# Token-major gate and output projections in the first block's mixers, with the merged result turned on TensorE

## The chip, the cores and the metric

One core of one Trainium2 chip. The metric is the device time of one execution in microseconds, as the median of a few runs. The kernel before was run three times: 1937.15 to 1938.6 us, median 1938.12 us.

## The reference

A model of 256 tokens and width 1024: two layers of a first block, then two of a second one. The change is in the mixer of the first block, so only that part is given:

```
h = rmsnorm(x, mix_norm_pre[l])
z = h @ w_in[l]
aq, ak, av, mq, mk, mv, mo, mi, mf, gl = jnp.split(z, SPLIT_IDX, axis=-1)
ya = diff_attention(aq, ak, av, lam, lam_init, attn_norm_w[l])
...
ym = (jax.nn.sigmoid(mo) * rmsnorm(hm, mlstm_norm_w[l]).reshape(b_, s_, M_V))
g_a, g_m = jnp.split(jax.nn.sigmoid(gl + gate_b[l]), 2, axis=-1)
merged = g_a * (ya @ w_proj_a[l]) + g_m * (ym @ w_proj_m[l])
x = x + rmsnorm(merged @ w_out[l], mix_norm_post[l])
```

`gl` is 256 x 2048, `ya`, `ym` and `merged` are 256 x 1024, and `hm` is the output of a chunkwise mLSTM with 8 heads of 128 values each.

## The kernel before

Every weight matrix is streamed through the core once, in 623 units of 128 x 1024 values (512 KB). SyncE loads a unit into a ring of four (`w_raw`). ScalarE rounds it into `w_hi` (line 572) and VectorE takes the rest, `w_raw` minus `w_hi`, into `w_lo` (line 1094); both rings hold six units. A matrix product is then three passes on TensorE: high part by high part, high by low and low by high. ScalarE splits unit u once unit u-6 is used up (`unit_done`), so the two splitting engines run up to five units ahead of TensorE.

There are two ways to use a unit.

- Feature-major (`product`, lines 1854 to 1856, called by `model_unit`): a 128 x 128 tile of the weights is loaded into the array and 256 tokens stream past. A unit is 24 matmuls of 256 columns, and its result, 128 features x 256 tokens, is finished in one unit, in a third of the way round three PSUM banks (`out_bank`).
- Token-major (`tokens`, lines 1860 to 1862, called by `chunk`): a 128 x 128 tile of the activations (128 tokens, 128 of the inner dimension) is loaded and 512 columns of weights stream past. A unit is 12 matmuls of 512 columns, and four units make a chunk: 512 features for the two halves of the tokens, in two banks (`tok_bank`).

A mixer is 88 units, numbered here 0 to 87 from its start, as the variable `i` of the loops in the code: values of the attention (0 to 7, token-major), queries, keys and convolution inputs (8 to 31, feature-major), output gate and values of the mLSTM (32 to 47, token-major), `gl` (48 to 63), `ya @ w_proj_a` (64 to 71) and `ym @ w_proj_m` (72 to 79), all 32 of them feature-major, and `merged @ w_out` (80 to 87, with `merged` as the array's side). In the listing these starts are `U_MO` 32, `U_GL` 48, `U_PA` 64, `U_PM` 72 and `U_OUT` 80.

Each engine has a program of its own, and its order is that of the `for i in range(U_QK, U_OUT)` loop in that engine's block. In its step i, TensorE first does the small work that is due (scores of mLSTM head (i-48)/2 on even i, values on odd i, the transposes of `ym_turn`), then unit i. ScalarE and VectorE split unit i+5 in their step i and do the small work that belongs to i. All waits are semaphores: an engine that waits holds up everything behind it in its own program.

The mLSTM heads run in three groups, 0 to 2, 3 to 5 and 6 and 7. For a group ScalarE copies the numerators out of PSUM (`take_num`, line 754) and squares them, VectorE computes denominators and variances (`mlstm_stats`), ScalarE the reciprocal root (`mlstm_rstd`), and VectorE scales the heads into `ym_tok` (`mlstm_out`, line 1394). There is one copy of `num`, so `take_num` of a group waits for the `ym_ready` of all heads before it. Then TensorE turns the heads two by two into bank 3 (`ym_turn`, line 2153), and ScalarE and VectorE split them out of it (`ym_round`, line 772; `ym_rest`, line 1404). `ym_turn(p)` waits until the pair before has left the bank (`ym_split`).

The gates are scaled by the row norm out of PSUM (line 1474), put through the sigmoid with a bias for each partition (line 836), multiplied with the projections (line 1412), added (1416) and split (843, 1418).

Of the kernel before, what the change touches and what calls it, by code (L numbers as in the profile page):

```python
# [5 lines left out]
F32 = mybir.dt.float32  # L6
# [37 lines left out]
for _name, _n in (("attn_norm", 1), ("one_minus_lam_init", 1), ("lam_init", 1),  # L44
                  ("mlstm_norm", HEADS), ("conv_w", 32), ("conv_b", 8), ("gate_b", 16), ("lam", 4),
                  ("igate_b", 1), ("fgate_b", 1), ("w_gates", KT * 64)):
    C1[_name] = _at
    _at += _n
# [10 lines left out]
NPAR = max(N1, N2)  # L59

# [13 lines left out]
NC = _at  # L74


def build(nc, x, consts, gains, params, w_up1, w_down1, w_mix1, w_mix2, w_up2, w_down2, out):
    with ExitStack() as ctx:
# [73 lines left out]
        gl, _ = sb("gates_merge", [P, 16, T])  # L152
# [191 lines left out]
        gl_scaled = sem("gl_scaled")  # L344
# [46 lines left out]
        proj_done = sem("proj_done")  # L391
# [57 lines left out]
        def conv_at(l):  # L449
# [4 lines left out]
        TOK_FIRST = (0, 4, U_MO, U_MO + 4, U_MV, U_MV + 4)  # L454
        tok_bank = ((bank[0], bank[1]), (side[0], side[1]), (bank[2], bank[0]), (bank[1], bank[2]),
                    (bank[0], bank[1]), (bank[2], bank[0]))
        GROUPS = ((0, 3), (3, 6), (6, 8))
        YA_TURN = (25, 27, 35, 37)
        YM_TURN = (57, 63, 65, 68)
# [86 lines left out]
        def _(act):  # L546
# [119 lines left out]
            def mixer(l):  # L666
# [3 lines left out]
                def store(c, dst):  # L670
                    for t in range(QT):
                        if t == 0:
                            act.wait_ge(chunk_out, l * 6 + c + 1)
# [100 lines left out]

                for j in range(8):
                    hi_next()
# [7 lines left out]
                for i in range(U_QK, U_OUT):  # L784
# [48 lines left out]
                    if 65 <= i < 69:  # L833
                        for m in range(4 * (i - 65), 4 * (i - 64)):
                            act.wait_ge(gl_scaled, l * 16 + m + 1)
                            nc.scalar.activation(gl[:, m], gl[:, m], ACT.Sigmoid,
                                                 bias=p1("gate_b", m)).then_inc(gl_sig, 1)
                    if i == 70:
                        exp_set()
                    if i >= U_PM:  # L840
                        m = i - U_PM
                        act.wait_ge(proj_done, l * 24 + 8 + 2 * (m + 1))
                        nc.scalar.activation(h_hi[:, m], gl[:, m], ACT.Copy).then_inc(mix_hi, 1)
                for i in range(U_OUT, U_MIX - 2):
                    hi_next()
                post_norm(n, u0 + U_MIX - 1, n + 1)
# [91 lines left out]
            def mixer2(l):  # L938
# [52 lines left out]
                def take_gelu(t):  # L991
                    if t == 0:
                        act.wait_ge(chunk_out, DEPTH * 6 + l * 2 + 1)
# [4 lines left out]
                def take_values(t):  # L998
                    if t == 0:
                        act.wait_ge(chunk_out, DEPTH * 6 + l * 2 + 2)  # L1000
# [51 lines left out]
            for l in range(DEPTH):  # L1052
                ffn(l, 0)

                act.wait_ge(par_in, l * 16 + 16)
                mixer(l)
                ffn(l, 1)
            for l in range(DEPTH):
                nc.scalar.preload_act_table_set("gelu_and_others")

                act.wait_ge(par_in, l * 16 + 16 * (DEPTH + 1))
# [7 lines left out]
        def _(dve):  # L1069
# [134 lines left out]
            def mixer(l):  # L1204
# [179 lines left out]
                def mlstm_out(g):  # L1384
# [7 lines left out]
                    for h in range(a, z):  # L1392
                        for t in range(QT):
                            r = nc.vector.scalar_tensor_tensor(
                                out=ym_tok[:, t, h * P:(h + 1) * P], in0=num[:, t, h - a, 0:P],
                                scalar=m_rs[:, t, h - a:h - a + 1], in1=mo_tok[:, t, h * P:(h + 1) * P],
                                op0=ALU.mult, op1=ALU.mult)
                        r.then_inc(ym_ready, 1)
# [9 lines left out]
                def proj(i):  # L1408
                    m = i - U_PA
                    dve.wait_ge(gl_sig, l * 16 + m + 1)  # L1410
                    dve.wait_ge(unit_done, u0 + i + 1)
                    nc.vector.tensor_tensor(gl[:, m], gl[:, m], out_bank(i), ALU.mult).then_inc(proj_done, 1)
                    if i >= U_PM:
                        m = i - U_PM
                        dve.wait_ge(proj_done, l * 24 + 8 + 2 * m + 1)
# [1348 lines left out]
```

## Time and profile before

| | before |
|---|---|
| median of 3 runs | 1938.12 us (1937.15 to 1938.6) |
| time of the profiled execution | 1937.21 us |
| its span | 1935.0 us |
| busy TensorE matmul, weight load, VectorE, ScalarE | 99%, 86%, 67%, 58% |
| units 48 to 79, first mixer | 356.95 to 465.77 us, 108.82 us |
| the same, second mixer | 1025.25 to 1134.0 us |
| granted TensorE clock, mean | 0.999 |

The span is what the profiler saw of the one execution, 2.2 us less than its time. All positions below are microseconds from the start of the span. 

The durations of matmul records overlap, since matmuls are pipelined. What a matmul costs is read from the distance between starts, not from its duration.

### The profile page before, as it was taken

Reading aid. Unit: us, or ns where it says so; the run is one execution under the profiler, and the core shown is the slowest. Engines: PE = TensorE matmul, PEld = TensorE weight load, DVE = VectorE, ACT = ScalarE, POOL = GpSimd, SP = SyncE. Lnnn points to the kernel's source line nnn. Section 1 sums busy time; section 2 is a strip of 40 time slices with the busy share of each in tenths; the row PEclk is TensorE's granted clock in tenths of the full one; section 3 lists DMA queues with packets and bytes.
Section 4 is the critical chain, followed back from the end, with each engine's and each line's share of the span. In section 5 each row is a group of like instructions: output and inputs, shape, how many; then the busy total and the mean of one; then the engine's idle time right before and its main releaser. Section 6 shows DMA issues by size and latency. Waiting matters only on the chain.

```text
span 1935.0 us, 28373 instructions
## 1 busy us (share of the span) xinstructions
PE 1922.7 (99%) x10936; PEld 1660.8 (86%) x10936; DVE 1303.2 (67%) x2243; ACT 1123.9 (58%) x1798; POOL 6.5 (0%) x18
## 2 busy tenths in 40 slices
PE   9999999999999999999999999999999999999998
PEld 7888899999888888888989998888988888988887
DVE  5555887566755575558865666555858888858886
ACT  6444766564644564456774655445747666647665
POOL 0000000000000000000000000000000000000000
PEclk9999999999999999999999999999999999999999
DMA  8655445546566555655455446664536555536553
GB/s 285 192 186 185 163 137 169 163 132 198 192 190 189 174 185 185 187 161 174 142 166 163 153 162 218 187 190 153 171 113 187 183 187 179 172 111 188 183 187 97
DMA packets 93684, 335.74 MB, mean 174 GB/s; under 512 B 10224, under 2 KB 12528, under 8 KB 93552
## 3 DMA queue, kind: packets, MB, share of 16 engines
q1 hardware_dynamic: 92688, 329.49, 54.1%
q0 software_dynamic: 720, 4.37, 0.6%
q8 instruction: 87, 1.43, 0.3%
q14 instruction: 45, 0.37, 0.1%
q10 hardware_dynamic: 144, 0.09, 0.0%
HBM read 332.86 MB, written 1.05 MB: 173 GB/s over the span
## 4 chain that ended last, share of the span: by engine, by line
PE 94%; DVE 5%; ACT 1%; issue 0%; DMA 0%; SPq 0%; DVEq 0%; ACTq 0%
PE stream L1860 10%; PE stream L1862 10%; PE stream L1861 10%; PE acc L1860 9%; PE acc L1862 9%; PE acc L1861 9%; PE stream L1854 7%; PE stream L2344 7%; PE stream L1855 7%; PE stream L1856 7%; PE stream L2345 3%; PE stream L1956 1%; DVE w_lo L1094 1%; PE acc L2270 1%; PE acc L2067 1%; DVE conv_tiles L1559 1%
## 5 line engine op out<-in xcount | busy, mean ns | idle before, releaser
L1094 DVE TENSOR_TENSOR w_lo<-w_raw,w_hi 128x1024 fp32r<-128x1024 f32 x623 | 757.9, 1223 | 363.6 <-ACT w_hi L572 362.1
L572 ACT ACTIVATE w_hi<-w_raw 128x1024 fp32r<-128x1024 f32 x623 | 653.4, 1054 | 372.5 <-PE stream L1862 206.8
L1860 PE MATMUL stream<-w_hi,h_both 128*128 128x512 f32 x896 | 354.0, 395 | 0.0
L1862 PE MATMUL stream<-w_lo,h_both 128*128 128x512 f32 x896 | 349.1, 390 | 0.0
L1861 PE MATMUL stream<-w_hi,h_both 128*128 128x512 f32 x896 | 348.9, 389 | 0.0
L1854 PE MATMUL stream<-h_both,w_hi 128*128 128x256 f32 x800 | 234.4, 293 | 0.0
L1856 PE MATMUL stream<-h_both,w_lo 128*128 128x256 f32 x800 | 226.0, 283 | 0.0
L1855 PE MATMUL stream<-h_both,w_hi 128*128 128x256 f32 x800 | 226.0, 283 | 0.0
L2344 PE MATMUL stream<-h_both,w_hi 128*128 128x512 f32 x608 | 217.4, 400 | 0.0
L1860 PE MATMUL acc<-w_hi,act_hi 128*128 128x512 f32 x528 | 211.2, 400 | 1.6 <-DVE conv_sums L1551 1.3
L1862 PE MATMUL acc<-w_lo,act_hi 128*128 128x512 f32 x528 | 206.3, 391 | 0.0
L1861 PE MATMUL acc<-w_hi,act_lo 128*128 128x512 f32 x528 | 206.0, 390 | 0.0
L1860 PEld LDWEIGHTS stream<-w_hi,h_both 128*128 128x128 f32 x896 | 168.3, 188 | 35.8 <-DVE w_lo L1094 1.0
L1862 PEld LDWEIGHTS stream<-w_lo,h_both 128*128 128x128 f32 x896 | 168.2, 188 | 35.6
L1861 PEld LDWEIGHTS stream<-w_hi,h_both 128*128 128x128 f32 x896 | 168.4, 188 | 33.1
L2345 PE MATMUL stream<-h_both,w_lo 128*128 128x256 f32 x608 | 170.7, 281 | 0.0
L1854 PEld LDWEIGHTS stream<-h_both,w_hi 128*128 128x128 f32 x800 | 152.8, 191 | 4.0 <-issue 0.8
L1855 PEld LDWEIGHTS stream<-h_both,w_hi 128*128 128x128 f32 x800 | 153.0, 191 | 0.1
L1856 PEld LDWEIGHTS stream<-h_both,w_lo 128*128 128x128 f32 x800 | 152.8, 191 | 0.0
L2344 PEld LDWEIGHTS stream<-h_both,w_hi 128*128 128x128 f32 x608 | 114.2, 188 | 26.9
L1860 PEld LDWEIGHTS acc<-w_hi,act_hi 128*128 128x128 f32 x528 | 99.2, 188 | 23.9 <-issue 2.6
L1862 PEld LDWEIGHTS acc<-w_lo,act_hi 128*128 128x128 f32 x528 | 99.1, 188 | 21.8
(336 smaller groups left out, 2614.7 us busy)
## 6 DMA issues: line engine op xcount, KB each, us to landing
w_raw<-in_w_up SPq DMA_DIRECT2D x264, 512.0 KB, 3.5
w_raw<-in_w_mix SPq DMA_DIRECT2D x228, 512.0 KB, 3.5
w_raw<-in_w_down SPq DMA_DIRECT2D x132, 512.0 KB, 3.5
params<-in_params POOLq DMA_DIRECT2D x4, 859.5 KB, 6.4
x_residual<-in_x SPq DMA_DIRECT2D x4, 256.0 KB, 5.6
out_x<-x_residual SPq DMA_DIRECT2D x4, 256.0 KB, 2.5
constants<-in_consts POOLq DMA_DIRECT2D x1, 832.0 KB, 7.2
constants<-in_consts SPq DMA_DIRECT2D x1, 192.0 KB, 8.0
```

Of the source, the lines that this page charges most:

```text
L572: nc.scalar.activation(w_hi[:, u % RING], w_raw[:, u % RAW], ACT.Copy).then_inc(hi_ready, 1)
L1094: nc.vector.tensor_tensor(w_lo[:, u % RING], w_raw[:, u % RAW], w_hi[:, u % RING].bitcast(F32), ALU.subtract).then_inc(split_done, 1)
L1559: r = nc.vector.scalar_tensor_tensor(out=cbuf[:, s, back:], in0=conv_src(i, side_i)[:, 0:T - back], scalar=p2("conv_w", ((2 - back) * 2 + ...
L1854: nc.tensor.matmul(dst, w_hi[:, s, w], hi, start=first, stop=False)
L1855: nc.tensor.matmul(dst, w_hi[:, s, w], lo, start=False, stop=False)
L1856: return nc.tensor.matmul(dst, w_lo[:, s, w], hi, start=False, stop=last)
L1860: nc.tensor.matmul(dst, hi, w_hi[:, s, w], start=first, stop=False)
L1861: nc.tensor.matmul(dst, lo, w_hi[:, s, w], start=False, stop=False)
L1862: return nc.tensor.matmul(dst, hi, w_lo[:, s, w], start=False, stop=last)
L1956: r = nc.tensor.transpose(dst, cbuf[:, 2 * (c % 2) + t, half(i)], ident)
L2344: nc.tensor.matmul(dst, w_hi[:, u % RING, w], h_both[:, k], start=(k == 0), stop=False)
L2345: r = nc.tensor.matmul(dst[:, 0:T], w_lo[:, u % RING, w], h_hi[:, k], start=False, stop=(k == KT - 1))
```

## The change

The 16 units of `gl`, the 8 of `w_proj_a` and the 8 of `w_proj_m` are packed as `wide` units on the host and used token-major: eight more chunks (6 to 13) of four units. `out_bank` is no more used for them, and chunk c takes the next two of banks 0 to 2. The results lie token-major in `gl`, so:

- VectorE takes each chunk in two pieces of 128 x 512, with a bias that now varies along the row (`gl_take`), which is loaded as 2 x 1024 values for each partition: half of it into `params`, half over constants that only the second block uses, which are loaded later. The first piece is taken when the first token half of the chunk is done (`chunk_out`, half way through the chunk's last unit), before VectorE's split in that step; the second one after it, with a wait for the unit's end.
- The sigmoid is four instructions of 128 x 1024 in steps 65, 67, 70 and 73, where there were 16 of 128 x 256 in steps 65 to 68.
- `merged` is token-major and `w_out` needs its transpose: eight 128 x 128 transposes ahead of unit 78 and eight ahead of unit 82 (`merged_turn`), each eight split by two ScalarE and two VectorE instructions.
- `mlstm_out` is called by head, in steps 55, 57, 61, 63 and 65, where it was called by group in 55, 61 and 65. The first two `ym_turn` move from 57 and 63 to 60 and 64, the third from 65 to 66.

```diff
-        YM_TURN = (57, 63, 65, 68)
+        HEADS_OUT = {55: (0,), 57: (1, 2), 61: (3, 4), 63: (5,), 65: (6, 7)}
+        SIGMOID_AT = (65, 67, 70, 73)
+        YM_TURN = (60, 64, 66, 68)
+        MERGE_TURN = (78, 82)
...
+                def gl_take(c, t):
...
+                    if t == 0:
+                        dve.wait_ge(chunk_out, l * TOK_CHUNKS + c + 1)
+                    else:
+                        dve.wait_ge(unit_done, u0 + TOK_FIRST[c] + 4)
+                    nc.vector.scalar_tensor_tensor(out=gl[:, t, cols_c], in0=tok_bank[c][t][:],
+                                                   scalar=rs_all[:, T + t:T + t + 1], in1=b, op0=ALU.mult,
+                                                   op1=ALU.add).then_inc(gl_taken, 1)
...
+                    taking = i >= U_GL and i % 4 == 3
+                    if taking:
+                        chunk_take(GL_CHUNK + (i - U_GL) // 4, 0)
                     lo_next()
+                    if taking:
+                        chunk_take(GL_CHUNK + (i - U_GL) // 4, 1)
...
-                        if i == U_GL + 3 + 2 * (z - 1):
-                            mlstm_out(g)
+                    if i in HEADS_OUT:
+                        for h in HEADS_OUT[i]:
+                            mlstm_out(h)
...
+                def merged_turn(a):
+                    for t in range(QT):
+                        pe.wait_ge(merged_in, l * 4 + 2 * a + t + 1)
...
+                        for j in range(4):
+                            r = nc.tensor.transpose(bank[3 - t][:, blk(j)],
+                                                    gl[:, t, (4 * a + j) * P:(4 * a + j + 1) * P], ident)
+                        r.then_inc(merged_turned, 1)
...
-                    if i < U_PA:
-                        model_unit(out_bank(i), u, h_hi, h_lo)
...
+                    model_unit(out_bank(i), u, h_hi, h_lo)
```

Three places show how the engines' programs change. The first is VectorE's program in steps 62 to 65 of the first mixer; before:

```order
L1358 SCALAR_TENSOR_TENSOR mlstm_p<-acc,decay 128x384 [waits num_ready,mlstm_qk,mw_ready]
L1474 TENSOR_TENSOR gates_merge<-stream,mix_rstd 128x256 [waits unit_done]
L1094 TENSOR_TENSOR w_lo<-w_raw,w_hi 128x1024 [waits hi_ready]
L1404 SCALAR_TENSOR_TENSOR ym_lo<-stream,params,ym_hi 128x256 [waits ym_hi_done] x2
L1474 TENSOR_TENSOR gates_merge<-stream,mix_rstd 128x256 [waits unit_done]
L1094 TENSOR_TENSOR w_lo<-w_raw,w_hi 128x1024 [waits hi_ready]
L1367 SCALAR_TENSOR_TENSOR mlstm_den<-mlstm_num 128x2x2 [waits num_taken]
L1371 TENSOR_TENSOR mlstm_den<-mlstm_den,e_cols 128x2x2 [waits dve_step]
L1374 RECIPROCAL mlstm_rec<-mlstm_den 128x2x2 [waits m_stat]
L1376 TENSOR_REDUCE mlstm_var<-mlstm_num_squares 128x2x2 [waits num_squared]
```

and the same place of the changed kernel, where `L1113` is the split, `L1442` the taking of a chunk's piece and `L1419` a head's scaling:

```order
L1377 SCALAR_TENSOR_TENSOR mlstm_p<-acc,decay 128x384 [waits num_ready,mlstm_qk,mw_ready]
L1442 SCALAR_TENSOR_TENSOR gates_merge<-stream,mix_rstd,constants 128x512 [waits chunk_out]
L1113 TENSOR_TENSOR w_lo<-w_raw,w_hi 128x1024 [waits hi_ready]
L1442 SCALAR_TENSOR_TENSOR gates_merge<-stream,mix_rstd,constants 128x512 [waits unit_done]
L1419 SCALAR_TENSOR_TENSOR ym_tok<-mlstm_num,mlstm_rs,out_gate_tok 128x128 x2
L1113 TENSOR_TENSOR w_lo<-w_raw,w_hi 128x1024 [waits hi_ready]
L1386 SCALAR_TENSOR_TENSOR mlstm_den<-mlstm_num 128x2x2 [waits num_taken]
L1390 TENSOR_TENSOR mlstm_den<-mlstm_den,e_cols 128x2x2 [waits dve_step]
L1393 RECIPROCAL mlstm_rec<-mlstm_den 128x2x2 [waits m_stat]
L1395 TENSOR_REDUCE mlstm_var<-mlstm_num_squares 128x2x2 [waits num_squared]
L1397 TENSOR_TENSOR mlstm_var<-mlstm_var,mlstm_rec 128x2x2 [waits m_stat]
L1400 TENSOR_TENSOR mlstm_var<-mlstm_var,mlstm_rec 128x2x2 [waits m_stat]
```

Head 5 is now scaled in step 63, behind both pieces of chunk 9, and the pair of `ym_lo` splits has moved from step 63 to behind the statistics of step 64 (its row follows the last one shown). The second place is ScalarE's program in steps 63 to 65; before:

```order
L754 ACTIVATE mlstm_num<-acc 128x260 [waits ym_ready,num_ready]
L754 ACTIVATE mlstm_num<-acc 128x260
L757 ACTIVATE mlstm_num_squares<-mlstm_num 128x2x256 [waits num_taken]
L772 ACTIVATE ym_hi<-stream,params 128x256 [waits ym_turned]
L772 ACTIVATE ym_hi<-stream,params 128x256
L572 ACTIVATE w_hi<-w_raw 128x1024 [waits unit_done,raw_full3]
L763 ACTIVATE mlstm_rs<-mlstm_var,eps_72 128x2x2 [waits m_stat]
L766 ACTIVATE mlstm_rs<-mlstm_rs 128x2x2 [waits act_step]
```

and after the change, where `L766` is the copy of the numerators, `L584` the split, `L775` and `L778` the reciprocal root and `L784` the rounding of a turned head:

```order
L766 ACTIVATE mlstm_num<-acc 128x260 [waits ym_ready,num_ready]
L766 ACTIVATE mlstm_num<-acc 128x260
L769 ACTIVATE mlstm_num_squares<-mlstm_num 128x2x256 [waits num_taken]
L584 ACTIVATE w_hi<-w_raw 128x1024 [waits unit_done,raw_full3]
L775 ACTIVATE mlstm_rs<-mlstm_var,eps_72 128x2x2 [waits m_stat]
L778 ACTIVATE mlstm_rs<-mlstm_rs 128x2x2 [waits act_step]
L784 ACTIVATE ym_hi<-stream,params 128x256 [waits ym_turned]
L784 ACTIVATE ym_hi<-stream,params 128x256
```

The rounding of heads 2 and 3 stood ahead of the wait for the variances and now stands behind it. The third place is TensorE's program at the start of unit 78 of the changed kernel, where nothing stood between units 77 and 78 before:

```order
L1924 MATMUL stream<-w_lo,ym_hi 128x512
L2242 MATMUL stream<-constants,gates_merge 128x128 [waits ym_split,merged_in]
L2242 MATMUL stream<-constants,gates_merge 128x128 x3
L2242 MATMUL stream<-constants,gates_merge 128x128 [waits merged_in]
L2242 MATMUL stream<-constants,gates_merge 128x128 x3
L1922 MATMUL stream<-w_hi,ym_hi 128x512 [waits split_done]
```

Eight transposes were put in, in two waits of four.

## Rows read from the trace of the kernel before

**Rows 1.** Page, part 1: busy time and share of the span by engine.

```profile
PE 1922.7 (99%) x10936; PEld 1660.8 (86%) x10936; DVE 1303.2 (67%) x2243; ACT 1123.9 (58%) x1798; POOL 6.5 (0%) x18
```

**Rows 2.** Page, part 4: the chain that ended last, by engine.

```profile
PE 94%; DVE 5%; ACT 1%; issue 0%; DMA 0%; SPq 0%; DVEq 0%; ACTq 0%
```

**Rows 3.** Windows: units 48 to 79, 40 to 46 (token-major), 69 to 76 (feature-major).

```profile
356.95:465.77 108.82, 108.82 (x889) 105.81 (x888) 69.20 (x126) 57.71 (x95) 0.00 (x0) 1.00 0.50 149
335.20:354.24 19.04, 19.04 (x86) 15.77 (x85) 8.49 (x7) 13.51 (x14) 0.00 (x0) 1.00 0.66 202
434.10:457.14 23.04, 23.04 (x195) 23.04 (x194) 16.34 (x25) 11.82 (x18) 0.00 (x0) 1.00 0.67 199
```

**Rows 4.** Timeline of TensorE: where steps 62 to 66 start.

```profile
410.77 0.34 PE L2116 MATMUL acc<-neg_keys_rounded,ident_rounded 128*128 128x384 f32 x1
...
414.86 0.38 PE L2139 MATMUL acc<-mlstm_v_tok,mlstm_p 128*128 128x130 f32 x2
...
421.73 0.60 PE L2153 MATMUL stream<-constants,ym_tok 128*128 128x128 f32 x4
...
425.03 0.28 PE L1854 MATMUL stream<-ya_hi,w_hi 128*128 128x256 f32 x1
```

**Rows 5.** Timeline of TensorE: 12 token-major matmuls with four, and with eight, transposes.

```profile
320.66 0.60 PE L2102 MATMUL stream<-constants,o_normed 128*128 128x128 f32 x4
...
323.84 0.39 PE L1860 MATMUL stream<-w_hi,h_both 128*128 128x512 f32 x1
...
485.52 0.39 PE L1860 MATMUL acc<-w_hi,h_both 128*128 128x512 f32 x1
...
489.15 0.39 PE L1860 MATMUL acc<-w_hi,h_both 128*128 128x512 f32 x1
```

**Rows 6.** Lines: VectorE's split, a 128x512 piece from PSUM, a head's scaling, mLSTM weights.

```profile
L1094 DVE TENSOR_TENSOR w_lo<-w_raw,w_hi 128x1024 fp32r<-128x1024 f32 x623 | 757.9, 1223 | 363.6 <-ACT w_hi L572 362.1
...
L1336 DVE SCALAR_TENSOR_TENSOR ya_lo<-stream,attn_norm_scaled,ya_hi 128x512 fp32r<-128x512 f32 x8 | 6.0, 748 | 7.8 <-ACT ya_hi L730 7.8
...
L1394 DVE SCALAR_TENSOR_TENSOR ym_tok<-mlstm_num,mlstm_rs,out_gate_tok 128x128 f32<-128x128 f32 x32 | 8.9, 346 | 0.2
...
L1358 DVE SCALAR_TENSOR_TENSOR mlstm_p<-acc,decay 128x384 f32<-128x384 f32 x16 | 8.8, 551 | 0.0
```

**Rows 7.** Timeline of ScalarE, steps 63 to 65.

```profile
416.08 0.65 ACT L754 ACTIVATE mlstm_num<-acc 128x260 f32<-128x260 f32 x2
...
417.30 0.82 ACT L772 ACTIVATE ym_hi<-stream,params 128x256 fp32r<-128x256 f32 x2
...
422.92 0.30 ACT L763 ACTIVATE mlstm_rs<-mlstm_var,eps 128x4 f32<-128x4 f32 x1 [2.76 <-DVE mlstm_var L1381]
...
423.36 1.04 ACT L572 ACTIVATE w_hi<-w_raw 128x1024 fp32r<-128x1024 f32 x1
424.31 0.82 ACT L772 ACTIVATE ym_hi<-stream,params 128x256 fp32r<-128x256 f32 x2
425.14 1.28 ACT L836 ACT_TABLE_LOAD   x1
```

**Rows 8.** Timeline of VectorE, steps 62 to 64.

```profile
415.06 0.42 DVE L1474 TENSOR_TENSOR gates_merge<-stream,mix_rstd 128x256 f32<-128x256 f32 x1 [0.64 <-PE stream L1856]
...
418.16 0.88 DVE L1404 SCALAR_TENSOR_TENSOR ym_lo<-stream,params,ym_hi 128x256 fp32r<-128x256 f32 x2 [0.72 <-ACT ym_hi L772]
...
420.20 1.23 DVE L1094 TENSOR_TENSOR w_lo<-w_raw,w_hi 128x1024 fp32r<-128x1024 f32 x1 [0.73 <-ACT w_hi L572]
421.34 0.16 DVE L1367 SCALAR_TENSOR_TENSOR mlstm_den<-mlstm_num 128x4 f32<-128x4 f32 x1
```

**Rows 9.** The span's end: TensorE's last transposes, then windows with the granted clock.

```profile
1929.36 1.23 PE L2265 MATMUL stream<-constants,y_tok 128*128 128x128 f32 x8 [2.79 <-ACT y_tok L864]
...
1929.50:1930.00 0.50, 0.50 (x6) 0.50 (x6) 0.00 (x0) 0.00 (x0) 0.00 (x0) 1.00 0.00 0
1930.00:1930.50 0.50, 0.50 (x5) 0.21 (x2) 0.00 (x0) 0.45 (x2) 0.00 (x0) 0.68 0.00 0
```

In the window rows the columns are: stretch, its length, busy time (and instructions) of TensorE, its weight load, VectorE, ScalarE and GpSimd, granted clock of TensorE, busy share of the DMA engines, GB/s. In the rows of lines: busy us in total, mean ns of one, idle time before them.

More of the change, by code:

```diff
@@ L773, in ym_round, with merged_round @@
                                              scale=p1("mlstm_norm", 2 * p + j)).then_inc(ym_hi_done, 1)
+                def merged_round(a):
+                    for t in range(QT):
+                        act.wait_ge(merged_turned, l * 4 + 2 * a + t + 1)
+                        nc.scalar.activation(h_hi[:, 4 * a:4 * a + 4, half(t)],
+                                             bank[3 - t][:].rearrange("p (k q) -> p k q", k=4),
+                                             ACT.Copy).then_inc(mix_hi, 1)
                 for j in range(8):
@@ L832, in mixer @@
                         ym_round(YM_TURN.index(i))
[L833 to L838, printed above, removed]
+                    if i in SIGMOID_AT:
+                        c = SIGMOID_AT.index(i)
+                        act.wait_ge(gl_taken, l * 16 + 2 * (c + 1))
+                        x = gl[:, :, 512 * c:512 * (c + 1)]
+                        nc.scalar.activation(x, x, ACT.Sigmoid).then_inc(gl_sig, 1)
+                    if i == SIGMOID_AT[-1] + 1:
                         exp_set()
[L840 to L843, printed above, removed]
+                    if i in MERGE_TURN:
+                        merged_round(MERGE_TURN.index(i))
                 for i in range(U_OUT, U_MIX - 2):
                     hi_next()
+                    if i in MERGE_TURN:
+                        merged_round(MERGE_TURN.index(i))
                 post_norm(n, u0 + U_MIX - 1, n + 1)
@@ L1391, in mlstm_out @@
                         dve.wait_ge(mo_ready, l + 1)
[L1392 to L1398, printed above, removed]
+                def mlstm_out(h):
+                    for g, (a, z) in enumerate(GROUPS):
+                        if h == a:
+                            mlstm_scales(g)
+                        if a <= h < z:
+                            at = h - a
+                    for t in range(QT):
+                        r = nc.vector.scalar_tensor_tensor(
+                            out=ym_tok[:, t, h * P:(h + 1) * P], in0=num[:, t, at, 0:P],
+                            scalar=m_rs[:, t, at:at + 1], in1=mo_tok[:, t, h * P:(h + 1) * P],
+                            op0=ALU.mult, op1=ALU.mult)
+                    r.then_inc(ym_ready, 1)
                 def ym_rest(p):
@@ new lines, in chunk_take, with merged_rest @@
+                def chunk_take(c, t):
+                    if c < PA_CHUNK:
+                        gl_take(c, t)
+                    else:
+                        proj_take(c, t)
+                def merged_rest(a):
+                    for t in range(QT):
+                        dve.wait_ge(mix_hi, l * 4 + 2 * a + t + 1)
+                        nc.vector.tensor_tensor(h_lo[:, 4 * a:4 * a + 4, half(t)],
+                                                bank[3 - t][:].rearrange("p (k q) -> p k q", k=4),
+                                                h_hi[:, 4 * a:4 * a + 4, half(t)].bitcast(F32),
@@ L2653, in mix1 @@
     heads = np.stack([tiles(a) for a in (q, k)], axis=1).reshape(2 * HEADS, P, D)
[L2654 to L2655 removed]
+    return np.concatenate([wide(va), heads, tiles(mqk)]
+                          + [wide(a) for a in (mo, mv, gl[:, 0:D], gl[:, D:], v["w_proj_a"][l], v["w_proj_m"][l])]
                           + [v["w_out"][l].reshape(KT, P, D)])
```

142 lines of the change are left out of this document (82 added, 60 removed).

## The prediction

> **What bounds the kernel now.** I read the page first: TensorE is busy 99% of the span, VectorE 67%, ScalarE 58% [rows 1], and the chain that ended last runs on TensorE for 94% [rows 2]. Then the windows of the changed place: in units 48 to 79 TensorE is busy for all of the 108.82 us at a granted clock of 1.00, VectorE for 69.2 and ScalarE for 57.7 of them, the DMA engines half the time [rows 3]. So TensorE never waits there, and the time moves in two ways only: by what TensorE is given to do, and by a wait that comes anew. VectorE and ScalarE have room, and work taken from them is worth nothing in itself. It is their order that counts.
>
> **Less matmul time.** A unit has 6144 columns in either form. Eight feature-major units took 23.04 us, 2.88 each; seven token-major ones took 19.04 us, 2.72 each [rows 3]. Per matmul that is 23.04 / 192 = 0.120 us for 256 columns and 19.04 / 84 = 0.227 us for 512: each costs some 13 ns more than its columns at 2.4 GHz, and a token-major unit has 12 fewer of them. 32 units in each of two mixers save 64 x 0.16 = 10.2 us.
>
> One rule speaks against this saving. The Trainium skill ("TensorE: Matmul & The Clock Gate", section "Wait — 56ns, not 53.3ns?") gives a warm matmul its columns over 2.4 GHz plus about 2.5 ns. By it the units would take 24 x 109.2 and 12 x 215.8 ns, 0.03 us apart, and the 64 would save 1.9 us in place of 10.2. The rows of this kernel decide, since both forms run here with the same operand types [rows 3].
>
> **New transposes.** The 16 transposes of a mixer come in two batches of eight. Twelve token-major matmuls with eight transposes among them took 489.15 - 485.52 = 3.63 us [rows 5], 0.91 more than 2.72. Four batches: +3.6 us. They turn another tile but are the same fp32 128 x 128 operation. By twice the cost of four transposes, below, a batch would be 0.84 to 0.92, so the bounds are 3.4 and 3.7.
>
> **Small work among larger matmuls.** Four transposes ahead of a unit cost 425.03 - 421.73 - 2.88 = 0.42 us in feature-major surroundings [rows 4] and 323.84 - 320.66 - 2.72 = 0.46 in token-major ones [rows 5]. 0.03 to 0.04 more at each of 20 places (eight scores, eight values, four head turns) in two mixers is +1.4; two fewer changes of form give some back. I take +1.0 (0 to 1.6).
>
> **What lies beside.** VectorE's two pieces of a chunk (748 ns each for such a shape [rows 6]) replace four of about 420 ns, four sigmoids replace 16, and the split of `merged` shrinks from eight instructions to four on either engine. None was waited for [rows 3], so all this is nothing. The added bias loads are 1 MB beside 336 MB, on GpSimd's queue, with a whole FFN to arrive in. The banks: a chunk's first piece is taken at the half of its last unit and its bank is needed 2.7 us later, and the split of turned results at unit 78 has until unit 80; both have more than a microsecond left.
>
> **The wait that comes anew.** In step 63 the changed order makes a ring. ScalarE's copy of the third group's numerators waits for head 5, and VectorE scales head 5 only after both pieces of chunk 9; and `ym_turn(2)` ahead of unit 66 waits for the split of heads 2 and 3, which now stands behind the third group's statistics on VectorE and behind its reciprocal root on ScalarE. Before, head 5 was ready in step 61 and the split of step 63 stood ahead of the statistics. The clock of the chain starts at 0 when the second half of unit 63 starts:
> - the signal reaches VectorE 0.20 later (415.06 after 414.86) [rows 4, 8]; first piece of chunk 9, 0.67 to the next start (748 ns long [rows 6], less the 0.08 by which the split's 1.23 exceeds the 1.14 to the next start [rows 8]); split of unit 68, 1.14; second piece, 0.67; head 5 in two instructions of 0.35 [rows 6], the first again 0.08 less: at 3.30 head 5 is ready
> - ScalarE starts 0.04 later; numerators and squares, 1.22 to the next start (416.08 to 417.30 [rows 7]); split of unit 69, 1.04 [rows 7]: 5.60
> - VectorE's half of unit 69 starts 0.04 later, 1.14; statistics up to ScalarE's root 1.58 (421.34 to 422.92 [rows 7, 8]): 8.36
> - root, 0.44 to the next start; rounding of two heads 0.82 [rows 7]; 0.04, and the rest of them 0.88 [rows 8]: 10.54.
>
> TensorE meanwhile needs 1.36 for the rest of unit 63, 0.46 for `ym_turn(1)` [rows 5] and 2 x 2.72: it stands before `ym_turn(2)` at 7.26. With 0.1 for the signal the wait is 10.64 - 7.26 = 3.4 us. It could be 2.6, if pieces and hand-overs run faster, or 4.2. Before, nothing of this was near: heads 0 to 5 were scaled in good time, and the wait for the variances (2.76 us on ScalarE [rows 7]) stood behind the rounding. Both mixers: +6.8 us (5.2 to 8.4). It does not spread: five units are split ahead of TensorE, and `ym_turn(3)` comes at 10.64 + 0.46 + 2 x 2.72 = 16.5. ScalarE is free at 8.36 + 0.44 + 0.82 = 9.6, and up to there it and VectorE need a split (1.04), a table load (1.28), a sigmoid of a split's size (1.04), a split (1.04), a rounding (0.82) and a rest (0.92) [rows 7, 8]: 15.8, 0.7 early.
>
> Another place is close. Head 4's weights must be ready for unit 57. From the half of unit 55 VectorE has 0.20, a piece 0.67, a split 1.14, a piece 0.67, head 0 with its small product 0.73, a split 1.14 and the weights 0.55 [rows 6, 8]: 5.1. TensorE has 1.36, and a scores step of 414.86 - 410.77 = 4.09 [rows 4] less 0.16: 5.3. I count no wait, with 0.3 in each mixer as the upper bound.
>
> **Sum.** -10.2 + 3.6 + 1.0 + 6.8 = +1.2 us on the profiled execution: a span of 1936.2 and a time of 1938.4. That execution's 1937.21 is 0.9 below the median of the runs, so the median goes from 1938.12 to 1939.3. The lower bounds together give 1936.5, the upper ones (3.7, 1.6, 8.4 and 0.6 for unit 57) 1942.2.
>
> **The rivals.**
> - *No wait.* The chain above is cut somewhere (ScalarE does not come to depend on head 5, say) and TensorE never stands at unit 66. Then -5.6: 1932.5. For it: TensorE did not wait at any place of these units before. Against: the chain is 3.3 us too long, all of its lengths but the pieces of chunk 9 come from this same stretch, and no step of it can be passed by an engine that keeps its order. To get below 1934.2 the wait must shrink under 0.9 us. Chance 0.10.
> - *The clock falls, slower.* At the span's end the last dense matmul ended about 1926.56, TensorE stood for 2.79 us, and eight transposes ran from 1929.36; the granted clock was 1.00 up to 1930.0 and 0.68 on average in the half microsecond after, so it went from 2.4 to 1.2 GHz about 3.6 us after the dense work ended [rows 9]. A wait of 3.4 us followed by four transposes is close to that. No row shows how long the lower clock would stay under dense work; as an estimate, if as long as it took to fall, half of 3.6 us is lost each time. One fall of the two: 1941.1; both: 1942.9, which is slower. It decides once TensorE is without dense matmuls for about as long as there, so from a wait of some 3.2 us with the four transposes behind it. Chance that it makes the kernel slower by more than 0.2%: 0.15; that one fall leaves it within: 0.25. The Trainium skill (same page, section "Why this matters for your kernels") advises against idle gaps between bursts of matmuls, since the clock goes back to its lower level; the end of this trace agrees.
> - *Columns alone count.* If a matmul's time were its columns, both forms of a unit would take 6144 / 2.4 GHz = 2.56 us, the change would save nothing on them, and the 3.6 + 1.0 + 6.8 would be left: 1949.5, slower. Against it stand the 2.88 and 2.72 us [rows 3]. Chance 0.01. The Trainium skill's rule above comes near to it, with 1947.6.
> - *More waits.* Unit 57 and `ym_turn(3)` both wait after all: 0.3 to 1 us each in each mixer, 1940 to 1943. Chance 0.06.
>
> **How the numbers follow.** A measurement of this kernel tells changes of over 0.2% (3.9 us) from none: faster is below 1934.2, slower above 1942.0. My forecast, with the wait at unit 66 and the clock kept or lost once at most, has 0.68. Faster: 0.10 of no wait and 0.01 of a short one, 0.11. Slower: 0.15 clock, 0.01 rule, 0.03 of more waits, 0.19. Same: 0.70. The range reaches down to the lower bounds of the terms, less the 1 us by which executions of one kernel differ, 1935.5, leaving out no wait (0.10), and up to both falls of the clock, 1943.3, leaving out under 0.05.
>
> **What would show it.** In the changed profile: token-major units of 2.72 us all through steps 48 to 79; two groups of eight transposes for each mixer costing 0.9; a wait of TensorE of about 3.4 us ahead of unit 66 in both mixers, ended by VectorE's rest of the turned heads, and ScalarE's copy of numerators waiting on VectorE's scaling of head 5; units 48 to 79 in about 108.82 - 5.1 + 0.9 + 0.5 + 3.4 = 108.5 us (the second batch of transposes is behind them). A granted clock under 1.00 there would be the second rival. The prediction is wrong if TensorE stands anywhere else for more than half a microsecond, or nowhere.

## The result and the profile after

The changed kernel takes 1943.53 us (median of 9 runs, 1941.71 to 1945.73), the kernel before beside it 1937.38 (9 runs, 1937.06 to 1938.6). The ratio is 1.003, with a 95% interval of 1.0022 to 1.0039: slower by 0.3%, past the 0.2% that the prediction took as the least that can be told. The difference is +6.2 us, where +1.2 was forecast. The time is 0.2 us above the upper end of the predicted range (1943.3), which the interval of the ratio takes in. The profiled execution took 1944.23, its span is 1942.4 (1935.0 before).

The page of the changed kernel, part 1, then part 4 by engine, beside [rows 1, 2]:

```profile
PE 1923.0 (99%) x10200; PEld 1627.1 (84%) x10200; DVE 1297.1 (67%) x2195; ACT 1119.5 (58%) x1766; POOL 8.1 (0%) x21
...
PE 91%; DVE 6%; ACT 1%; issue 1%; DMA 0%; DVEq 0%; ACTq 0%
```

736 matmuls fewer, and yet TensorE is busy for as long as before (1922.7). By the prediction's own terms for its work (-10.2, +3.6, +1.0) it would be busy for 5.6 us less, so this is the first hint at a slower clock. The waits of TensorE over the whole span (engine, tile and line waited for; us in total, times, longest):

```profile
PE stream L2220 <- DVE ym_lo L1429: 6.5, 2, 3.2
PE stream L2334 <- ACT y_tok L883: 3.3, 4, 2.8
PE stream L2622 <- DVE ln_half L1840: 1.5, 1, 1.5
PE acc L1922 <- DVE conv_sums L1610: 1.3, 2, 0.7
PE acc L2511 <- DVE qk L1732: 1.0, 2, 0.7
```

The first row is new, one wait in each mixer, at `ym_turn(2)` ahead of unit 66. The last one was a single wait of 0.12 us before. The others stood in the kernel before with the same sizes. Windows of the changed kernel: units 48 to 79 of the first and of the second mixer (columns as in [rows 3]), where it was 108.82 us in both [rows 3]:

```profile
357.38:467.94 110.56, 107.32 (x513) 87.18 (x512) 66.44 (x104) 55.68 (x80) 0.00 (x0) 0.98 0.48 153
1028.22:1139.89 111.67, 108.43 (x513) 88.16 (x512) 66.45 (x104) 55.68 (x80) 0.00 (x0) 0.97 0.47 152
```

Less work (TensorE was busy for all 108.82), and the granted clock is under 1.00. Where it is lost, the shorter windows show, behind the wait in the first mixer and then in the second, where the first row ends within the wait and the next one lies wholly in it:

```profile
423.00:426.60 3.60, 0.36 (x4) 0.30 (x4) 2.13 (x7) 2.54 (x6) 0.00 (x0) 1.00 0.45 146
426.60:428.00 1.40, 1.40 (x8) 1.18 (x7) 1.36 (x4) 1.39 (x2) 0.00 (x0) 0.75 0.00 0
428.00:430.00 2.00, 2.00 (x6) 1.56 (x5) 1.16 (x4) 2.00 (x4) 0.00 (x0) 0.50 0.67 225
430.00:432.00 2.00, 2.00 (x8) 1.58 (x8) 1.57 (x3) 0.87 (x2) 0.00 (x0) 0.82 0.25 66
...
1093.00:1096.20 3.20, 0.92 (x5) 0.42 (x3) 1.73 (x8) 1.33 (x5) 0.00 (x0) 1.00 0.51 161
1096.20:1096.80 0.60, 0.00 (x0) 0.00 (x0) 0.60 (x2) 0.60 (x1) 0.00 (x0) 0.60 0.04 14
...
1101.00:1103.00 2.00, 2.00 (x6) 1.58 (x5) 1.41 (x3) 0.09 (x1) 0.00 (x0) 0.50 0.27 55
1103.00:1105.00 2.00, 2.00 (x10) 1.59 (x10) 0.20 (x1) 1.58 (x2) 0.00 (x0) 0.96 0.58 229
```

0.50 is 1.2 GHz. In the first mixer the clock fell about 1 us after the work had begun again (426.33) and was low for 3.4 us; in the second it fell 0.84 us before TensorE could go on (1097.16), and was low for 6.8 us:

```profile
427.31:430.72 3.41, 3.41 (x10) 2.64 (x9) 2.54 (x8) 2.94 (x5) 0.00 (x0) 0.50 0.45 154
1096.32:1103.15 6.83, 5.99 (x16) 4.88 (x17) 5.14 (x11) 4.74 (x6) 0.00 (x0) 0.50 0.31 92
```

The timeline of TensorE shows what that does to a matmul of 512 columns: 0.43 from start to start where it is 0.23 at 2.4 GHz.

```profile
422.70 0.39 PE L1924 MATMUL stream<-w_lo,ya_hi 128*128 128x512 f32 x1
426.33 0.63 PE L2220 MATMUL stream<-constants,ym_tok 128*128 128x128 f32 x4 [3.24 <-DVE ym_lo L1429]
426.71 0.48 PE L1922 MATMUL stream<-w_hi,ya_hi 128*128 128x512 f32 x1
...
428.91 0.63 PE L1922 MATMUL stream<-w_hi,ya_hi 128*128 128x512 f32 x1
429.33 0.63 PE L1923 MATMUL stream<-w_hi,ya_lo 128*128 128x512 f32 x1
...
431.14 0.39 PE L1922 MATMUL stream<-w_hi,ya_hi 128*128 128x512 f32 x1
431.37 0.39 PE L1923 MATMUL stream<-w_hi,ya_lo 128*128 128x512 f32 x1
```

The wait itself is the ring that the prediction followed. Its links, from the chain of the changed kernel that ended last (start, us, what):

```profile
415.81 0.75 DVE gates_merge L1442
416.56 1.13 DVE w_lo L1113
417.69 0.66 DVE gates_merge L1442
418.35 0.53 DVE ym_tok L1419 x2
...
418.93 0.04 issue
418.97 0.68 ACT mlstm_num L766 x2
...
420.21 1.05 ACT w_hi L584
421.26 0.02 issue
421.29 1.22 DVE w_lo L1113
...
423.81 0.17 DVE mlstm_var L1400
424.01 0.31 ACT mlstm_rs L775
...
424.81 0.47 ACT ym_hi L784
425.28 0.03 issue
425.31 0.89 DVE ym_lo L1429 x2
```

The second half of unit 63 began at 415.61, so the last row ends some 10.6 after it (predicted 10.54), and the matmul ahead of the wait would have handed over at 422.70 + 0.23 = 422.93, 3.40 before the transposes start (predicted 3.4). ScalarE's copy of the numerators (`L766`) waited 4.09 us for head 5, as foretold.

### The profile page after: what moved, and what is told of

Same layout as the page of the kernel before. It is cut to its first block, busy times and chain, and to the rows that moved or that the text cites. A ratio compares the mean times of both kernels' runs of the same rounds, so it can differ in the third digit from the quotient of the medians.

```text
span 1942.4 us, 26766 instructions
## 1 busy us (share of the span) xinstructions
PE 1923.0 (99%) x10200; PEld 1627.1 (84%) x10200; DVE 1297.1 (67%) x2195; ACT 1119.5 (58%) x1766; POOL 8.1 (0%) x21
## 4 chain that ended last, share of the span: by engine, by line
PE 91%; DVE 6%; ACT 1%; issue 1%; DMA 0%; DVEq 0%; ACTq 0%
PE stream L1922 13%; PE stream L1924 12%; PE stream L1923 12%; PE acc L1922 9%; PE acc L1924 9%; PE acc L1923 9%; PE stream L2413 7%; PE stream L2414 3%; PE stream L1916 3%; PE stream L1917 3%; PE stream L1918 3%; DVE w_lo L1113 2%; PE stream L2018 1%; PE acc L2339 1%; PE acc L2134 1%; DVE conv_tiles L1618 1%
## 5 line engine op out<-in xcount | busy, mean ns | idle before, releaser
L1113 DVE TENSOR_TENSOR w_lo<-w_raw,w_hi 128x1024 fp32r<-128x1024 f32 x623 | 758.8, 1222 | 380.0 <-ACT w_hi L584 378.2
L584 ACT ACTIVATE w_hi<-w_raw 128x1024 fp32r<-128x1024 f32 x623 | 654.5, 1055 | 412.5 <-PE stream L1924 292.3
L1922 PE MATMUL stream<-w_hi,h_both 128*128 128x512 f32 x1024 | 407.1, 398 | 0.0
L1924 PE MATMUL stream<-w_lo,h_both 128*128 128x512 f32 x1024 | 399.4, 390 | 0.0
L1923 PE MATMUL stream<-w_hi,h_both 128*128 128x512 f32 x1024 | 398.7, 389 | 0.0
L1922 PEld LDWEIGHTS stream<-w_hi,h_both 128*128 128x128 f32 x1024 | 192.4, 188 | 41.3 <-DVE w_lo L1113 0.9
L1924 PEld LDWEIGHTS stream<-w_lo,h_both 128*128 128x128 f32 x1024 | 192.2, 188 | 41.1
L1923 PEld LDWEIGHTS stream<-w_hi,h_both 128*128 128x128 f32 x1024 | 192.5, 188 | 37.3
L2414 PE MATMUL stream<-h_both,w_lo 128*128 128x256 f32 x608 | 170.7, 281 | 0.0
L1916 PE MATMUL stream<-h_both,w_hi 128*128 128x256 f32 x544 | 159.1, 292 | 0.0
L1917 PE MATMUL stream<-h_both,w_hi 128*128 128x256 f32 x544 | 153.7, 283 | 0.0
L1918 PE MATMUL stream<-h_both,w_lo 128*128 128x256 f32 x544 | 153.7, 283 | 0.0
L2413 PEld LDWEIGHTS stream<-h_both,w_hi 128*128 128x128 f32 x608 | 114.2, 188 | 26.9
L2414 PEld LDWEIGHTS stream<-h_both,w_lo 128*128 128x128 f32 x608 | 114.9, 189 | 0.8
L1923 PEld LDWEIGHTS acc<-w_hi,act_lo 128*128 128x128 f32 x528 | 99.4, 188 | 17.8
L1916 PEld LDWEIGHTS stream<-h_both,w_hi 128*128 128x128 f32 x544 | 104.0, 191 | 2.0 <-issue 0.8
```

Source lines behind the costliest of these rows:

```text
L584: nc.scalar.activation(w_hi[:, u % RING], w_raw[:, u % RAW], ACT.Copy).then_inc(hi_ready, 1)
L1113: nc.vector.tensor_tensor(w_lo[:, u % RING], w_raw[:, u % RAW], w_hi[:, u % RING].bitcast(F32), ALU.subtract).then_inc(split_done, 1)
L1916: nc.tensor.matmul(dst, w_hi[:, s, w], hi, start=first, stop=False)
L1917: nc.tensor.matmul(dst, w_hi[:, s, w], lo, start=False, stop=False)
L1918: return nc.tensor.matmul(dst, w_lo[:, s, w], hi, start=False, stop=last)
L1922: nc.tensor.matmul(dst, hi, w_hi[:, s, w], start=first, stop=False)
```

## The experiments

The theory: the changed kernel is 6 us slower because of the ring through head 5, which takes 3.4 us of TensorE in each mixer, and because each such stand also costs the clock; without it the change would gain. The rivals: the order is innocent and the chunks' pieces, the forms or the transposes cost more than reckoned; or the clock falls for another reason than the stand. Each kernel was timed beside the kernel before on its chip (medians there 1937.56 to 1937.66). What tells most is one number from the traces, the length of units 48 to 79:

```
                       first   second mixer   TensorE's stands there (first / second)
before                108.82   108.82         none
after                 110.56   111.67         3.24 / 3.24
k1_head5              105.99   106.06         0.31 / 0.30
k2_turn63             110.48   111.54         3.24 / 3.23
k3_fill               108.88   108.94         1.43 / 1.43  (behind 8 filling matmuls)
k4_order_only         110.38   110.38         0.67 + 0.58, both
k5_both               105.88   105.88         0.27 / 0.27
k6_fill3              108.93   110.55         2.57 / 2.57  (behind 3 filling matmuls)
k8_turn_twice         106.78   106.81         0.25 / 0.24
k9_form_proj          107.91   107.88         none
k10_form_all          109.65   109.65         none
```

**k1_head5.** One head out earlier cuts the ring at its first link.

```diff
-        HEADS_OUT = {55: (0,), 57: (1, 2), 61: (3, 4), 63: (5,), 65: (6, 7)}
+        HEADS_OUT = {55: (0,), 57: (1, 2), 61: (3, 4, 5), 65: (6, 7)}
```

> The changed kernel with head 5 scaled in step 61 (with heads 3 and 4) and not in step 63. Nothing else. Theory (the ring of step 63 and the clock that falls behind it cost the time): ScalarE's copy of the last group's numerators no longer waits for VectorE, the chain to the rest of heads 2 and 3 ends 7.6 us after the half of unit 63 where it ended at 10.6, TensorE waits 0.3 to 0.5 us ahead of unit 66 in place of 3.4, and the granted clock is 1.00 all through both mixers. Time 1933.5 to 1935.5 us. Rival (the time is lost elsewhere, in the token-major form or its transposes, and the wait is only where it shows): the gain is at most the 6 us of the waits, 1938 us or more. Rival (the clock falls for another reason than the wait): the clock stays below 1.00 after unit 66 and the time is about 1938.

Measured: 1933.93 us (1932.51 to 1934.4), ratio 0.998 (0.9971 to 0.999). The wait ahead of unit 66 is 0.31 and the clock 1.00 in both stretches:

```profile
357.68:463.67 105.99, 105.68 (x514) 85.97 (x513) 66.24 (x104) 55.54 (x80) 0.00 (x0) 1.00 0.48 159
1023.98:1130.04 106.06, 105.76 (x514) 85.96 (x512) 66.27 (x104) 55.54 (x80) 0.00 (x0) 1.00 0.48 159
```

So one entry of a table is worth 9.6 us against the changed kernel, 4.6 and 5.6 in the two stretches. The waits grew shorter by 2.9 each. The rest, 1.6 and 2.7, is the clock's: it was below 1.00 in both stretches of the changed kernel and is 1.00 here.

**k2_turn63.** The second turn one step earlier, head 5 left where the change put it.

```diff
-        YM_TURN = (60, 64, 66, 68)
+        YM_TURN = (60, 63, 66, 68)
```

> The changed kernel with the turn of heads 2 and 3 ahead of unit 63 and not of unit 64, so that their split stands ahead of the last group's statistics, as before the change; head 5 stays in step 63. Theory of the ring: no wait ahead of unit 66. But ScalarE stays late by its wait for head 5, and the next pair (rounded after unit 71's split and a sigmoid) is out of the bank 15.7 us after the half of unit 63, where TensorE comes to the turn of heads 6 and 7 at 13.2: the wait moves to unit 68 and is about 2.6 us, in both mixers. Without a fall of the clock 1939 us, with one or two 1941 to 1943. Rival (only the order of the split matters, not head 5): no wait at all, 1933 to 1934 us.

Measured: 1942.78 us (1941.23 to 1944.91), ratio 1.0028 (1.0016 to 1.004). The third turn is in time now, and the fourth waits instead, two units later and just as long:

```profile
432.75 0.41 PE L2220 MATMUL stream<-constants,ym_tok 128*128 128x128 f32 x2 [3.24 <-DVE ym_lo L1429]
```

I had expected 2.6. The stand was moved, not shortened: the cause is the late head, not the turn behind which it shows. The clock fell again in both mixers (stretches 110.48 and 111.54).

**k3_fill and k6_fill3.** Eight matmuls of 512 columns (three in k6_fill3) into a bank that is free at that time stand ahead of `ym_turn(2)`. They shorten TensorE's idle time and leave the ring alone.

```diff
+                        if i == 66:
+                            for _ in range(8):
+                                nc.tensor.matmul(side[0][:, 0:512], ya_hi[:, 0, 0:P],
+                                                 ya_hi[:, 0:2].rearrange("p k t -> p (k t)"), start=True, stop=True)
```

> The changed kernel with eight more matmuls of 512 columns (some 1.8 us, into a free bank, their result is overwritten) ahead of the turn before unit 66, inside the wait. The wait's end does not move, only TensorE's idle time falls from 3.2 to about 1.4 us. Theory (the clock is lost through the idle time, and costs what the time lies above 1940): the granted clock is 1.00 through units 48 to 79 in both mixers, the wait still ends at the same place, and the time falls by 3 to 5 us, to 1939 to 1941 us. Rival (the lower clock is not due to the idle time, or costs nothing): the time stays at 1943 us, or rises.

> The changed kernel with three filling matmuls ahead of the turn before unit 66 in place of eight, so that TensorE idles about 2.6 us in each mixer (3.2 without filling, 1.4 with eight). It asks where between 1.4 and 3.2 us the clock begins to fall. Theory (a fall needs about the 3.6 us without dense matmuls of the trace's end): no fall in most executions, 1939.5 to 1940.5 us. Rival (the fall starts soon after 1.4 us of idle time): the clock is below 1.00 in one of the mixers at least, and the time is 1941 us or more.

Measured: 1939.7 us (1938.82 to 1940.22) with eight, ratio 1.0011 (1.0001 to 1.002); 1941.15 (1939.14 to 1942.32) with three, ratio 1.0016 (1.0006 to 1.0025). With eight TensorE idles for 1.43 us, the transposes start as long after the ring began as in the changed kernel, and the clock stays at 1.00 in both stretches:

```profile
357.06:465.94 108.88, 107.45 (x521) 87.56 (x520) 66.27 (x104) 55.54 (x80) 0.00 (x0) 1.00 0.48 156
1026.35:1135.29 108.94, 107.51 (x522) 87.55 (x520) 66.26 (x104) 55.55 (x80) 0.00 (x0) 1.00 0.48 155
```

That is 3.8 us back for work that has no use. The slowest of its ten executions (1940.22) is still faster than the fastest of the changed kernel's nine (1941.71), so probably none of those nine kept the clock in both mixers, though only one of them has a profile. With three TensorE idles for 2.57, and the one profiled execution has both answers, the clock kept in the first mixer and lost in the second (stretches 108.93 and 110.55):

```profile
428.00:431.00 3.00, 3.00 (x15) 2.48 (x14) 2.15 (x5) 3.00 (x5) 0.00 (x0) 1.00 0.53 175
...
1097.00:1099.00 2.00, 2.00 (x6) 1.54 (x5) 1.16 (x5) 2.00 (x3) 0.00 (x0) 0.50 0.59 137
1099.00:1101.00 2.00, 2.00 (x7) 1.59 (x7) 1.85 (x3) 0.87 (x3) 0.00 (x0) 0.67 0.31 125
```

I had expected no fall in most executions and 1939.5 to 1940.5 us; the rival, a fall in one mixer at least and 1941 or more, came true. The spread of its runs (1939.14 to 1942.32) would fit a kernel that loses the clock sometimes. The clock's share is shown by the changed kernel and k3_fill side by side: same order, same ring, the wait ended by the same instruction at the same place, and only the idle time differs.

**k4_order_only.** The kernel before, feature-major as it was, with the new steps for heads and turns alone.

```diff
-        YM_TURN = (57, 63, 65, 68)
+        YM_TURN = (60, 64, 66, 68)
+        HEADS_OUT = {55: (0,), 57: (1, 2), 61: (3, 4), 63: (5,), 65: (6, 7)}
...
-                        if i == U_GL + 3 + 2 * (z - 1):
-                            mlstm_out(g)
+                    if i in HEADS_OUT:
+                        for h in HEADS_OUT[i]:
+                            mlstm_out(h)
```

> The kernel before, feature-major, with the new order of the mLSTM outputs alone: heads scaled in steps 55, 57, 61, 63 and 65, turns ahead of units 60, 64, 66 and 68. Theory (the ring comes from this order, not from the token-major form): by the same steps, with the short evictions of this form, the rest of heads 2 and 3 ends 8.4 us after unit 63 where TensorE stands at 6.2: a wait of about 2.3 us ahead of unit 66 in both mixers, 1942 to 1943 us, the clock at 1.00. Rival (the ring needs the chunk's two pieces on VectorE): no wait, 1938 us.

Measured: 1940.83 us (1940.33 to 1941.35), ratio 1.0016 (1.0007 to 1.0025). Two waits in each mixer, ahead of units 66 and 68, of 0.67 and 0.58 us where I had put 2.3. VectorE's timeline shows why:

```profile
416.27 1.22 DVE L1095 TENSOR_TENSOR w_lo<-w_raw,w_hi 128x1024 fp32r<-128x1024 f32 x1 [0.73 <-ACT w_hi L573]
417.42 0.61 DVE L1401 SCALAR_TENSOR_TENSOR ym_tok<-mlstm_num,mlstm_rs,out_gate_tok 128x128 f32<-128x128 f32 x2
418.66 0.42 DVE L1482 TENSOR_TENSOR gates_merge<-stream,mix_rstd 128x256 f32<-128x256 f32 x1 [0.63 <-PE stream L1864]
```

Here head 5 (`L1401`) stands ahead of the piece that waits for unit 63 (`L1482`), in the changed kernel behind two such pieces and the wait for the unit's end. So the order alone makes a ring of a microsecond; with the pieces of the chunk ahead of the head it makes 3.4. Neither part has it by itself.

**k5_both.** Both moves, head 5 in step 61 and the second turn in step 63.

> The changed kernel with both moves: head 5 scaled in step 61, and the turn of heads 2 and 3 ahead of unit 63. Theory: the rest of heads 2 and 3 is out of the bank 3.5 us after the half of unit 63 and of heads 4 and 5 12.8 us after it, where TensorE comes to its turns at 7.3 and 13.2: no wait ahead of unit 66 or 68, the clock at 1.00, and the time is that with head 5 alone moved (1933.9) less its two waits of 0.45: about 1933 us, 0.2 to 0.3% below the kernel before. Rival (the saving of the token-major form is smaller than 10 us and what was gained came from elsewhere): 1936 us or more.

Measured: 1933.94 us (1932.99 to 1934.74), ratio 0.998 (0.9972 to 0.9989). I had expected no wait and about 1933 us. There is one of 0.27 ahead of unit 68, and the kernel is no better than k1_head5. It is the base of the four kernels that follow.

**k7_bias_late.** Changed kernels reach step 48 of the first mixer 0.1 to 1.0 us later than before. Is that the added bias load at the start? Its second half waits for unit 24 here.

```diff
                     if k == 0:
+                        pool.wait_ge(unit_done, 24)
```

> The kernel with both moves, and the first layer's second half of the gate bias (512 KB) loaded only when 24 units are used up, not at 25 us. All of the changed kernels' traces are 0.4 us late from unit 8 on. Theory (this load disturbs the first weight loads): the 0.4 us are gone, 1932.6 us. Rival (the first microseconds differ from execution to execution): the trace's first units are as in any of the others, no change in the median.

Measured: 1934.02 us (1933.1 to 1934.61), ratio 0.9979 (0.997 to 0.9988), and still 0.35 late at step 48. The 1932.6 us that I had expected without the disturbance did not come: the load is not the cause. k3_fill, with the load where the change put it, is 0.11 late, k2_turn63 1.01. The lateness comes in two parts: 0.04 to 0.6 us in the first units of the span, and in k1_head5, k2_turn63, k6_fill3 and k9_form_proj 0.3 to 0.6 more at unit 9 of the first mixer, where TensorE waits in some of them for ScalarE's `attn_v_tok`. With one profiled execution of each kernel, what differs between executions and what between kernels can't be told apart.

**k8_turn_twice.** k5_both with each eight transposes of `merged` done twice.

```diff
-                        for j in range(4):
+                        for j in (0, 1, 2, 3, 0, 1, 2, 3):
```

> The kernel with both moves, with every transpose of the merged result done twice into the same place: 32 more transposes. Theory (a batch of eight costs 0.9 us of which 0.1 is the change of form, and nothing else hangs on it): 4 x 0.8 = 3.2 us more than the kernel with both moves, about 1936.2 us. Rival (the first batch holds up more than its length, since units 80 and 84 wait for it): 5 us more or above.

Measured: 1937.78 us (1936.25 to 1938.45), ratio 0.9999 (0.999 to 1.0008), 3.8 above k5_both. In the traces the stretch, which holds one of the two batches, is 0.90 longer (106.78 against 105.88): four batches, 3.6. I had expected 3.2, with a tenth of a batch's 0.9 put down to the change of form; hardly any of it is.

**k9_form_proj and k10_form_all.** The largest term by itself: k5_both with the units multiplied feature-major again, out of the same units and into the same banks, 64 to 79 in the first, 48 to 79 in the second.

```diff
+                    for k in range(4 * t, 4 * t + 4) if c >= PA_CHUNK else ():
...
+                        dst = tok_bank[c][j // 2][:, j % 2 * 256:j % 2 * 256 + 256]
+                        r = product(dst, u % RING, k, hi[:, k], lo[:, k], k == 0, k == KT - 1)
```

> The kernel with both moves of the order (1933.94), but the 16 projection units of each mixer (64 to 79) are multiplied as feature-major ones: 24 matmuls of 256 columns in place of 12 of 512, out of the same units and into the same banks, with the same signals. The products are then not those of the reference (the unit's values are read as another matrix). By the distances between starts (2.88 against 2.72) 32 units cost 32 x 0.16 = 5.1 more, and the wait of 0.27 ahead of unit 68 goes (-0.5 in both mixers): 1938.5, between 1938.2 and 1939.3. By the rival, columns alone, nothing comes back: 1933.5 to 1934. By the rule of the Trainium skill in the first part of the prediction (0.03 for a unit) it would be 1934.4 to 1934.9.

> The same for all 32 units 48 to 79 of each mixer (gates and projections), with the products again not those of the reference. The form gives 64 x 0.16 = +10.2. The small work among the units (eight scores, eight values, four turns of heads) is then among matmuls of 256 columns again. By the sizes read in the changed kernel's trace it costs 0.05 less at each of 20 places, 2.0 in both mixers, and the wait of 0.27 ahead of unit 68 goes (0.5): 1941.6, between 1941.2 and 1942.2. By the prediction's term for that work (+1.0 for both mixers) it would be 1942.6. Against the run with the projections alone: +3.3 by the first, +4.3 by the second.

Measured: 1938.62 us (1937.0 to 1939.72), ratio 1.0005 (0.9996 to 1.0013), and 1940.93 (1940.22 to 1941.98), ratio 1.0018 (1.0009 to 1.0027). That is 4.7 and 7.0 above k5_both (4.6 and 7.7 expected; k10_form_all is 0.3 below its range). The traces are sharper than the medians; the first mixer's stretch, of k5_both, k9_form_proj and k10_form_all:

```profile
357.26:463.14 105.88, 105.61 (x513) 86.02 (x512) 66.08 (x104) 55.45 (x80) 0.00 (x0) 1.00 0.50 160
```

```profile
357.67:465.58 107.91, 107.91 (x706) 96.23 (x704) 66.18 (x104) 55.56 (x80) 0.00 (x0) 1.00 0.50 157
```

```profile
357.40:467.05 109.65, 109.65 (x897) 106.64 (x896) 66.22 (x104) 55.57 (x80) 0.00 (x0) 1.00 0.49 155
```

Sixteen projection units in the wide form are worth 2.03 us, and k9_form_proj has lost the wait of 0.27 besides, so some 2.4 by the form; the sixteen gate units, each of which has a scores or a values step ahead of it, are worth 1.74 and not 2.56. Columns alone is out, since by it nothing would come back. The rule of the Trainium skill that the prediction weighed ("TensorE: Matmul & The Clock Gate", section "Wait — 56ns, not 53.3ns?"), some 2.5 ns for each matmul over its columns, would give back 0.5 for sixteen units. It is out for these matmuls too.

## Why the prediction was right or wrong

- **Less matmul time, -10.2: right.** Token-major units between others of their kind take 2.72 us all through, in both mixers, and k9_form_proj and k10_form_all give the gain back when the form is undone.
- **New transposes, +3.6: right.** 0.90 for a batch in k8_turn_twice.
- **Small work among larger matmuls, +1.0 (0 to 1.6): too small, it is 1.9.** k10_form_all minus k5_both is 3.77 us for a stretch, with 5.12 of form in it; the other 1.35 is the wait of 0.27, with some 0.15 of restart (k4_order_only is 1.56 longer for 1.25 of waits), and 0.93 of small work. Twenty places, so 0.047 each, where I had read 0.03 to 0.04 from one pair of rows for the turns. The scores and values I had not seen in these surroundings.
- **What lies beside, nothing: right for the banks, the pieces, the sigmoids and the splits.** No wait of TensorE came from any of them in the mixers. Unit 57 was in time, and so was `ym_turn(3)`.
- **The new wait, +6.8 (5.2 to 8.4): right.** In place, cause, length (3.40 of 3.4) and both mixers; k1_head5 removes it by its first link.
- **The clock: this is the step that failed.** The prediction named the mechanism and the place, gave one fall a chance of 0.25 and two with a slower kernel 0.15, and left the clock out of the sum. It fell in all four stands of 3.24 us that profiles show (after and k2_turn63). The price was an estimate of 1.8 for a fall, from a low clock of 3.6 us; it was low for 3.4 and 6.8, and against the same stretch with the clock kept (108.9 in k3_fill and k6_fill3) that is 1.65 in the first mixer and 2.75 in the second. k2_turn63, with the same lengths of stand, has the same lengths of low clock; why they differ between the mixers no run shows. With 1.2 + 4.4 + 0.9 the sum would have been +6.5, and the span grew by 7.4.
- **What was not in the sum:** 0.43 us before step 48 of the first mixer (above, it varies), and 0.8 in the second block. There TensorE waits 0.34 and 0.65 (0.12 once before) for the last step of VectorE's work on `qk`, which stands behind a split of a unit that comes later: ScalarE waits 1.55 us for its load where it waited 0.41. The waits are there in all other kernels, together 0.2 to 1.0 us, and k4_order_only, feature-major as before, has one of 0.26, so the new form is not needed for them. Why the load is later is open; no run was aimed at it. The prediction had called itself wrong if TensorE stood anywhere else for more than half a microsecond. Units 48 to 79 have no such stand; the 0.65 here, outside them, is one.

The error was one of weighing. I had written that a stand of 3.4 us was close to the one at the end of the trace, after which the clock fell, and that it decides from about 3.2. My own central value for the wait was past that bound. Then the fall was the forecast and no rival. Its number for both falls, 1942.9, is 0.6 us from the median, but partly by luck: it stands on a median before of 1938.12, where nine runs gave 1937.38. As a change it was +4.8 against the measured +6.2; it lacks 0.9 of small work, 1.0 of the second fall's price and what was not in the sum. What made me hold it back was that the one row of a fall came 3.6 us after the dense work; in the second mixer it came about 1 us sooner (by the window of 0.60, some 2.6 us behind the dense work), in the first nearly 1 us later.

The size of k4_order_only was missed for another reason: I had priced the ring with head 5 behind the gates' piece, and in that kernel's code it stands ahead of it.

## What to carry to other kernels

When a wait of some microseconds comes upon a TensorE that has run dense, count the clock with it: here 3.4 us of standing cost 5.1 and 6.2. Order is to be followed link by link over all engines when work is re-timed: one head scaled two steps later, behind a piece that waits for the end of a unit, turned a gain of 3.7 us (k1_head5, k5_both) into a loss of 6.2. And a table of steps is the cheapest thing to try: the same change with head 5 in step 61 is faster than both kernels, 1933.93 against 1937.66 and 1943.53.

## What the runs showed of the hardware

- With idle times of 1.43 us the clock was kept both times, at 2.57 it was kept once and lost once, at 3.24 lost four times out of four. The lower clock lasted 3.4 us after one stand and 6.8 after the other, so stands alike to 0.01 us cost 1.65 and 2.75 us more, and the clock fell 1 us after the one and within the other. The Trainium skill ("TensorE: Matmul & The Clock Gate", section "Why this matters for your kernels") warns of idle gaps between bursts of matmuls. The falls here, at 2.57 and 3.24 us, agree.
- A mean over the span hides it: the granted clock was 0.997, and part 2 of the page shows no slice that differs. Only windows of 1 to 3 us show the 0.50.
- Filling matmuls without use made the kernel 3.8 us faster (k3_fill), by the clock alone.
- Eight fp32 transposes of 128 x 128 take 0.90 us among matmuls of 512 columns and 0.87 among those of 256 (unit 78 of k9_form_proj, 3.75 where a unit is 2.88).
